# One weight load for high and low dt weights, and squares added on GpSimd ahead of one product of ones

## The chip, the cores and the metric

The kernel runs on one core of a Trainium2 chip. The metric is the device time of one execution in microseconds. Its matrix engine is called TensorE (PE in the profile), its other engines VectorE (DVE), ScalarE (ACT), GpSimd (POOL) and SyncE (SP), which issues most of the DMAs.

## The reference

Two transformer-like blocks run one after the other on 256 tokens of width 1024, in fp32. The first has sliding-window attention, a gated recurrent branch and a gated feed-forward. The second is where the change lies:

```python
h = rmsnorm_2(x, norm_mix_w) * (1 + sc_m) + sh_m
z, xbc, dt_raw, q, k, v = jnp.split(h @ w_in, IN_SPLITS_2, axis=-1)   # 512, 1024, 8, 512, 512, 512 columns
xbc = silu(causal_dwconv(xbc, conv_w) + conv_b)
dt = softplus(dt_raw + dt_bias)                                       # 8 heads
y = ssd_scan(xs * dt[..., None], dt * A, bm, cm) + d_skip[:, None] * xs
y = y.reshape(b, s, 512) * silu(z)
y_ssd = rmsnorm_2(y, norm_w)        # y * rsqrt(mean(y * y over 512) + eps) * norm_w
y_att = chunk_attention(q, k, v, rel_bias)
x = x + g_m * (concatenate([y_ssd, y_att]) @ w_out)
h = rmsnorm_2(x, norm_ffn_w) * (1 + sc_f) + sh_f
x = x + g_f * conv_ffn(h, w_up, ffn_conv_w, w_down)
```

## The kernel before

Activations stand with their channels on the partitions ("cm" tiles) and 256 tokens along the free dimension. Every large product is split into high and low parts: a weight block `w` is held as `wH`, its value rounded to the fp32r type by ScalarE, and `wL = w - wH`, made by VectorE (`L1073`, the helper `tt`). Activations are held alike, `p1H` and `p1L`. TensorE then adds three products, `wH*p1H + wH*p1L + wL*p1H` (`L1672`, `L1675`), in one bank of its accumulator memory `ps`.

Weights come in panels of four blocks of 128 rows and 512 columns. SyncE loads them into four `raw` slots, ScalarE writes `wH` (`L695`), VectorE `wL`, TensorE multiplies. A panel is split two panels ahead of its use. One list written out by hand, `timeline()`, sets the order of the work; each engine walks through it and emits its own share of each entry, with semaphores between the engines. Within an engine the order is that of its queue.

The stretch that matters runs `xs`, `bc`, `q2`, `z`, `k2`, `v2`, `oo` for the second block. Between the panels of the groups stand the smaller steps:

```python
before_evac = {"oo1": [("squares", 3)], "xs": [("dt",)], "bc": [("xdt",)]}
gemm("xs", [("h_final",)])
gemm("bc", [("dt_turn",)])
gemm("q2", [("sA", 0)], [("sC", 0), ("sA", 1)])
gemm("z", [("sY", 0), ("sC", 1)], [("sY", 1), ("yz",)])
gemm("k2", [("ysum",), ("bias",), ("snorm",)], X(6, "k2", 1))
```

*dt.* `dtw` holds the 8 dt columns of `w_in_2` for the eight 128-row blocks. In `setup` ScalarE makes `dtH` and VectorE `dtL`. In `dt`, behind the second panel of `xs`, TensorE adds 8 x 3 products into 8 partitions of bank 7 (`L1893`). VectorE copies them to `dtrow` (`L1523`). In `dt_turn`, behind the first panel of `bc`, TensorE transposes `dtrow` into two 128x8 tiles (`L1899`). VectorE and ScalarE compute softplus and `ADT = dt * A` (semaphore `adt`; `L1033`, `L1035` on ScalarE). In `xdt`, behind the second panel of `bc`, TensorE waits for the convolved `xs` (`xc_done`, ScalarE `L901`) and `adt` and then transposes `xs` (`L1601`). The next group, `q2`, writes to the banks that ScalarE empties in its evacuation of `bc` (`L820`). The convolution of `xs` is twelve VectorE instructions (`L1076`) behind `L1523` in VectorE's queue.

*The SSD norm.* In `yz` VectorE multiplies the four 128x256 tiles of `y` by `silu(z)`, and ScalarE squares each into `sT[:, t]` (`L1043`, semaphore `ysq`). In `ysum`, behind the first panel of `k2`, TensorE adds the squares over partitions and tiles by four products with a matrix of ones (`L1951`, plain fp32, so that each product appears as two passes). ScalarE takes logarithm and exponential (`L1047`, `L1049`). In `snorm` VectorE multiplies, ScalarE and VectorE make the high and low parts for `oo`. The attention scores of unit 6 (`L1800`) stand behind the second panel of `k2`; they wait for the evacuation of `k2` on ScalarE.

GpSimd makes masks and constants at the start (`step` is its helper: the instruction raises `pool_step` and the next waits for it) and later does one product and one memset for each half of the recurrent branch (`L658`, `L666`).

Of the kernel before, what the change touches and what calls it, by code (L numbers as in the profile page):

```python
# [6 lines left out]
F32 = mybir.dt.float32  # L7
F32R = mybir.dt.float32r
BF16 = mybir.dt.bfloat16
U32 = mybir.dt.uint32  # L10
ACT = mybir.ActivationFunctionType
ALU = mybir.AluOpType
AX_X = mybir.AxisListType.X

P = 128
D = 1024
KD = D // P
T = 256
# [74 lines left out]
SUM_AT = {"f3": (2, 1), "f5": (3, 1), "f7": (4, 1), "f9": (5, 1), "norm": (6, 2), "post": (8, 2)}  # L93
SUMS = list(SUM_AT)
NSUM = 32
GATE_OF = {1: 0, 3: 1}

LATER = {("down1", 5): 2, ("oo1", 1): 3}
# [99 lines left out]
def build(nc, IN, out):  # L198
# [17 lines left out]
    with ExitStack() as ctx:  # L216


        on = Signals()
# [175 lines left out]
        def sb(name, shape, dt=F32):  # L395
            return ctx.enter_context(nc.sbuf_tensor(name, shape, dt))
# [57 lines left out]
        UT = sb("UT", [P, P], BF16)  # L454
        reset = sb("reset", [P, T], BF16)
        R0, R1, Ra, Rb = (sb(n, [P, TB]) for n in ("R0", "R1", "Ra", "Rb"))
        dtrow = scr(58, T)[0:8]
        XS, YS, S2, pre = sb("XS", [P, 2, TB]), sb("YS", [P, 2, TB]), sb("S2", [P, TB]), sb("pre", [P, TB])
        XA, YA, pre2 = sb("XA", [P, 1]), sb("YA", [P, 1]), sb("pre2", [P, 1])
        fetch, fetch2 = sb("fetch", [P, 32]), sb("fetch2", [P, 1])  # L460
# [7 lines left out]
        am, af = sb("am", [P, 8]), sb("af", [P, 8])  # L468
        RM, NM, DS, ES, SU, RD = (sb(n, [P, 2, 8]) for n in ("RM", "NM", "DS", "ES", "SU", "RD"))
        E5 = sb("E5", [P, 4, 4])  # L470
        dtH, dtL = sb("dtH", [P, KD, 8], F32R), sb("dtL", [P, KD, 8], F32R)
        DT, DR, DA, DE, ADT = (sb(n, [P, TB, 8]) for n in ("DT", "DR", "DA", "DE", "ADT"))
        nega, Bs = sb("nega", [P, 8]), sb("Bs", [P, 6, 8])
        ext_dram = nc.dram_tensor("ext_dram", (8, 384), F32).ap()
# [129 lines left out]
        @block.gpsimd  # L604
        def _(pool):

            steps = [0]

            def step(ins):

                steps[0] += 1
                ins.then_inc(on.pool_step, 1)
                pool.wait_ge(on.pool_step, steps[0])

            def select(t, cond, fill, op=ALU.is_ge):

                base_, mult, stp = cond
                step(pool.affine_select(out=t, in_=t, compare_op=op, fill=fill, base=base_,
                                        pattern=[[stp, t.shape[-1]]], channel_multiplier=mult))

            step(pool.memset(eps[:], EPS))
            step(pool.memset(nega[:], 0.0))
            step(pool.memset(ident[:], 0.0))
            select(ident[:], (0, 1, -1), 1.0, ALU.not_equal)
            step(pool.memset(ones[:], 1.0))

            step(pool.memset(identb[:], 0.0))
            select(identb[:], (0, 1, -1), 1.0, ALU.not_equal)

            step(pool.memset(mask1[:], 0.0))  # L630
            select(mask1[:, 0:P], (-1, -1, 1), NEG)
            select(mask1[:, P:2 * P], (0, 1, -1), NEG)

            step(pool.memset(reset[:], 1.0))
            step(pool.memset(reset[:, 0:T:C], 0.0))

            step(pool.memset(UT[:], 1.0))
            select(UT[:], (0, -1, 1), 0.0)
            step(pool.tensor_copy(CL[:], UT[:]))
            step(pool.memset(CL[0:C, C:P], 0.0))  # L640
            step(pool.memset(SL[:], 1.0))
            select(SL[:], (-1, 1, -1), 0.0)
            step(pool.memset(OL[:], 0.0))
            step(pool.memset(OL[0:C, :], 1.0))
            step(pool.memset(M0[:], 0.0))
            step(pool.tensor_scalar(M0[:, 0:C], CL[:, 0:C], -1.0, None, ALU.mult))
            step(pool.memset(M1[:], 0.0))
            step(pool.tensor_scalar(M1[:, C:P], CL[:, C:P], -1.0, None, ALU.mult))
            step(pool.tensor_copy(M1[0:C, 0:C], SL[0:C, 0:C]))

            step(pool.tensor_copy(hmask[0:C, :], UT[0:C, 0:C]))
            step(pool.tensor_copy(hmask[C:P, :], UT[C:P, C:P]))
            pool.memset(fetch2[:], 0.0).then_inc(on.consts, 1)
            for e in TL:
                if e[0] == "hprep" and e[2] == 2:
                    pool.wait_ge(on.hE3, e[1] + 1)
                    pool.wait_ge(on.hQp, e[1] + 1)
                    pool.tensor_tensor(hQ, hQ, T2, ALU.mult).then_inc(on.hQq, 1)  # L658
                elif e[0] == "hprep" and e[2] == 3:
                    if e[1]:  # L660
                        pool.wait_ge(on.o_psum, 2 * e[1])
                    else:
                        pool.wait_ge(on.aks, 2)
                        pool.wait_ge(on.dtw_lo, 1)
                        pool.wait_ge(on.pv_psum, NU1)
                    pool.memset(hAT, 0.0).then_inc(on.hat_zero, 1)  # L666
# [3 lines left out]
        def _(act):  # L670
# [241 lines left out]
            for e in TL:  # L912
# [26 lines left out]
                    tail(e[1])  # L939
                elif k == "setup":  # L940
                    act.wait_ge(on.in_dtw, 16)
                    nc.scalar.activation(dtH[:], dtw, ACT.Copy).then_inc(on.dtw_hi, 1)
                elif k == "scores":
                    table(ACT.Exp)
                elif k == "scale":
# [115 lines left out]
        def _(dve):  # L1061
# [10 lines left out]
            def tt(o, a, b, op):  # L1072
                return v.tensor_tensor(o, a, b, op)  # L1073
# [272 lines left out]
            for e in TL:  # L1346
# [21 lines left out]
                elif k == "setup":  # L1368
# [4 lines left out]
                    step(v.memset(ext[:, 0:P - 1], 0.0))  # L1373
                    v.tensor_scalar(ext[:, 0:P - 1], ext[:, 0:P - 1], ext[:, P - 1:P], None, ALU.add).then_inc(on.ext_done, 1)
                    dve.wait_ge(on.dtw_hi, 1)
                    tt(dtL[:], dtw, dtH[:].bitcast(F32), ALU.subtract).then_inc(on.dtw_lo, 1)
                elif k == "ada":
                    q = e[1]
                    i = SIDX["ada", q]
# [140 lines left out]
                elif k == "dt":  # L1520
                    dve.wait_ge(on.h_final, TB)
                    dve.wait_ge(on.dt_raw, 1)
                    v.tensor_copy(dtrow, ps[0:8, 7, 0:T]).then_inc(on.dt_row, 1)  # L1523
                elif k == "dt_turn":
                    dve.wait_ge(on.dt_psum, 1)
                    f = lambda n: pc(n, 0, 8).unsqueeze(1).broadcast_to([P, TB, 8])
# [70 lines left out]
        def _(pe):  # L1597
# [137 lines left out]
            for e in TL:  # L1735
# [152 lines left out]
                elif k == "dt":  # L1888
                    pe.wait_ge(on.dtw_lo, 1)
                    pe.wait_ge(on.u_ready, 24)  # L1890
                    for kk in range(KD):
                        for x, (wt, at_) in enumerate(((dtH, p1H), (dtH, p1L), (dtL, p1H))):
                            last = mm(ps[0:8, 7, 0:T], wt[:, kk, :], at_[:, kk, :], start=kk == 0 and x == 0,  # L1893
                                      stop=kk == KD - 1 and x == 2)
                    last.then_inc(on.dt_raw, 1)
                elif k == "dt_turn":
                    pe.wait_ge(on.dt_row, 1)
                    for j in range(TB):
                        last = nc.tensor.transpose(ps[:, 7, 8 * j:8 * j + 8], dtrow[:, j * P:(j + 1) * P], ident[0:8, 0:8])  # L1899
                    last.then_inc(on.dt_psum, 1)  # L1900
                elif k == "xdt":
                    pe.wait_ge(on.xc_done, 1)
# [5 lines left out]
                elif k == "sA":  # L1908
                    g = e[1]
                    pe.wait_ge(on.adt, 1)  # L1910
                    if g:
                        pe.wait_ge(on.seg, g)
                    a = sc45.rearrange("p (h n) -> p h n", h=4)
                    for h in range(4):
                        for j in range(TB):
                            last = mm(a[:, h, j * P:(j + 1) * P], ADT[:, j, 4 * g + h:4 * g + h + 1].broadcast_to([P, P]),
                                      CL[:], start=True, stop=True)
                    last.then_inc(on.abc_psum, 1)
                    pe.wait_ge(on.xd, 2)
                    if g == 0:  # L1920

                        for x, terms in enumerate((((M0, 0),), ((M1, 0),), ((SL, 0),), ((SL, 0), (OL, 1)),
                                                   ((M0, 1),), ((M1, 1),))):
                            for y, (mat, j) in enumerate(terms):
                                last = mm(ps[:, 7, 64 + 8 * x:72 + 8 * x], mat[:], ADT[:, j, :], start=y == 0,
                                          stop=y == len(terms) - 1)
                        last.then_inc(on.bm_psum, 1)
                elif k == "sC":
                    g = e[1]
                    if g:  # L1930
                        pe.wait_ge(on.cb, g)
                    pe.wait_ge(on.xc_done, 2)
                    mm(ps[:, 6, 0:T], XC[:, 4 + g, 0:P], XC[:, 6 + g, :], start=True, stop=True)
                    last = mm(ps[:, 6, T:T + P], XC[:, 4 + g, P:T], XC[:, 6 + g, P:T], start=True, stop=True)
                    last.then_inc(on.cb_psum, 1)
                elif k == "sY":
                    g = e[1]
                    pe.wait_ge(on.g_done, g + 1)
                    if g:
                        pe.wait_ge(on.sy, 2 * g)  # L1940
                    for hh in range(4):
                        h = 4 * g + hh
                        o = ps[C * (hh % 2):C * (hh % 2) + C, 7, (hh // 2) * T:(hh // 2 + 1) * T]
                        mm(o, XD[:, 0, h * DH:(h + 1) * DH], SG[g][:, hh, 0:T], start=True, stop=False)
                        last = mm(o[:, P:T], XD[:, 1, h * DH:(h + 1) * DH], SG[g][:, hh, T:T + P], start=False, stop=True)
                    last.then_inc(on.sy_psum, 1)
                elif k == "ysum":
                    pe.wait_ge(on.sy, 4)
                    for t in range(4):
                        pe.wait_ge(on.ysq, t + 1)  # L1950
                        last = mm(ysum, ones[:], sT[:, t], start=t == 0, stop=t == 3)  # L1951
                    last.then_inc(on.yss, 1)


INPUTS = ["x", "w_in", "b_in", "w_branch_attn", "w_branch_hgrn", "w_out", "w_ffn_gate", "w_ffn_up", "w_ffn_down",
# [40 lines left out]
```

## Time and profile before

| | |
|---|---|
| median of three runs | 815.47 us (815.34 to 817.68) |
| profiled execution | 815.34 us, its span 813.6 us |
| TensorE busy | 796.6 us, 98% |
| VectorE busy | 592.4 us, 73% |
| ScalarE busy | 498.6 us, 61% |
| GpSimd busy | 15.8 us, 2% |
| DMA moved | 161.15 MB |

The span runs from the first to the last instruction of the profiled execution. Times of rows are microseconds from its start. An instruction's row gives start, length, engine, source line, operation, output and inputs, shape and count; in brackets stands how long the engine was idle before it, and who ended that.

### The profile page before, as it was taken

How to read it: one execution, taken by the hardware profiler on the slowest of the kernel's cores; microseconds unless marked ns; L12 is line 12 of the kernel's file. 1: busy time of each engine (PE TensorE's matmuls, PEld its weight loads, DVE VectorE, ACT ScalarE, POOL GpSimd, SP SyncE). 2: the span in 40 equal slices, each digit the busy share in tenths (PEclk: the TensorE clock that was granted, in tenths of full speed). 3: DMA queues.
4: the chain of work that ended last, by engine and by line, in shares of the span. 5: the costliest groups of instructions: out<-in, count | busy, mean ns of one | idle time of the engine just before them, and what ended most of it. 6: DMA issues, size and time to landing. Idle time of an engine off the chain costs nothing. (4 is left out here: it accounts for less than half of the span.)

```text
span 813.6 us, 14276 instructions
## 1 busy us (share of the span) xinstructions
PE 796.6 (98%) x5952; PEld 744.8 (92%) x5952; DVE 592.4 (73%) x772; ACT 498.6 (61%) x752; POOL 15.8 (2%) x36
## 2 busy tenths in 40 slices
PE   8999999999999999999999999999999999999996
PEld 8988879999999889999998889999788999999885
DVE  5575686648766877887878897897768877787463
ACT  6777788568837475344344266856657776666452
POOL 3000000000200000000000000000000000000000
PEclk9999999999999999999999999999999999999999
DMA  8873634446453577889798993635352865646611
GB/s 301 285 252 111 207 104 156 155 155 226 162 183 105 160 254 232 264 292 298 253 300 279 354 358 110 234 133 155 104 173 68 256 205 168 197 137 200 233 52 52
DMA packets 105680, 161.15 MB, mean 198 GB/s; under 512 B 4480, under 2 KB 51856, under 8 KB 105616
## 3 DMA queue, kind: packets, MB, share of 16 engines
q1 hardware_dynamic: 105472, 159.97, 59.8%
q8 instruction: 47, 0.77, 0.4%
q10 hardware_dynamic: 144, 0.26, 0.1%
q14 instruction: 17, 0.14, 0.0%
HBM read 159.16 MB, written 1.06 MB: 197 GB/s over the span
## 5 line engine op out<-in xcount | busy, mean ns | idle before, releaser
L1073 DVE TENSOR_TENSOR wL<-raw,wH 128x2048 fp32r<-128x2048 f32 (+2 forms) x134 | 283.0, 2118 | 122.7 <-ACT wH L695 119.2
L1672 PE MATMUL ps<-p1H,wH 128*128 128x256 f32 x1256 | 359.2, 286 | 1.7 <-DVE p1L L1073 0.8
L1672 PE MATMUL ps<-p1L,wH 128*128 128x256 f32 x1256 | 355.3, 283 | 0.0
L1672 PE MATMUL ps<-p1H,wL 128*128 128x256 f32 x1256 | 355.3, 283 | 0.0
L695 ACT ACTIVATE wH<-raw 128x2048 fp32r<-128x2048 f32 (+1 forms) x120 | 223.1, 1866 | 122.1 <-PE ps L1672 65.9
L1672 PEld LDWEIGHTS ps<-p1H,wH 128*128 128x128 f32 x1256 | 240.8, 192 | 4.8 <-issue 3.5
L1672 PEld LDWEIGHTS ps<-p1L,wH 128*128 128x128 f32 x1256 | 240.9, 192 | 0.3 <-issue 0.2
L1672 PEld LDWEIGHTS ps<-p1H,wL 128*128 128x128 f32 x1256 | 240.8, 192 | 0.0
L1675 PE MATMUL ps<-wH,zH 128*128 128x512 f32 x168 | 65.4, 389 | 0.0
L1675 PE MATMUL ps<-wH,zL 128*128 128x512 f32 x168 | 65.4, 389 | 0.0
L1675 PE MATMUL ps<-wL,zH 128*128 128x512 f32 x168 | 65.4, 389 | 0.0
L1076 DVE SCALAR_TENSOR_TENSOR arena<-arena,par 128x256 f32<-128x256 f32 x124 | 50.7, 480 | 9.9 <-ACT arena L886 7.6
L820 ACT ACTIVATE arena<-ps 128x256 f32<-128x256 f32 x86 | 30.5, 378 | 28.2 <-PE ps L1672 27.8
L1076 DVE SCALAR_TENSOR_TENSOR arena<-raw,cact,arena 128x512 f32<-128x512 f32 x56 | 42.1, 751 | 1.7
L1073 DVE TENSOR_TENSOR arena<-arena 128x512 f32<-128x512 f32 (+3 forms) x41 | 35.2, 872 | 6.6 <-ACT arena L841 2.6
L1675 PEld LDWEIGHTS ps<-wL,zH 128*128 128x128 f32 x168 | 31.5, 188 | 6.6
L1675 PEld LDWEIGHTS ps<-wH,zH 128*128 128x128 f32 x168 | 31.5, 188 | 6.6
L1675 PEld LDWEIGHTS ps<-wH,zL 128*128 128x128 f32 x168 | 31.5, 188 | 6.4
L1672 PE MATMUL ps<-pyH,wH 128*128 128x256 f32 x128 | 36.6, 286 | 0.0
L1672 PE MATMUL ps<-pyL,wH 128*128 128x256 f32 x128 | 36.2, 283 | 0.0
L1672 PE MATMUL ps<-pyH,wL 128*128 128x256 f32 x128 | 36.2, 283 | 0.0
L1675 PE MATMUL ps<-wH,p1H 128*128 128x512 f32 (+1 forms) x92 | 34.4, 374 | 0.0
(284 smaller groups left out, 974.5 us busy)
## 6 DMA issues: line engine op xcount, KB each, us to landing
raw<-in_w_in SPq DMA_DIRECT2D x37, 1024.0 KB, 5.1
raw<-in_w_ada SPq DMA_DIRECT2D x24, 1024.0 KB, 5.2
raw<-in_w_up SPq DMA_DIRECT2D x44, 512.0 KB, 4.8
raw<-in_w_ffn_gate SPq DMA_DIRECT2D x22, 512.0 KB, 4.5
raw<-in_w_ffn_up SPq DMA_DIRECT2D x22, 512.0 KB, 5.6
raw<-in_w_ffn_down SPq DMA_DIRECT2D x10, 1024.0 KB, 5.3
raw<-in_w_down SPq DMA_DIRECT2D x10, 1024.0 KB, 5.0
raw<-in_w_out SPq DMA_DIRECT2D x8, 1024.0 KB, 5.1
```

Of the source, the lines that this page charges most:

```text
L695: nc.scalar.activation(wH[:, q % NHL, 0:nk, 0:wd], raw[:, i % NRAW, 0:nk, 0:wd], ACT.Copy).then_inc(on.w_hi, 1)
L820: nc.scalar.activation(dst(m), ps[:, t[1], 0:T], f, **bias).then_inc(on.evac_act, 1)
L1073: return v.tensor_tensor(o, a, b, op)
L1076: return v.scalar_tensor_tensor(out=o, in0=a, scalar=s, in1=b, op0=op0, op1=op1)
L1672: last = mm(ps[:, t[1], 0:T], wt[:, slot, k, t[2]:t[2] + P], at_[:, k0 + k, :], start=st, stop=en)
L1675: last = mm(ps[:, t[1], 0:t[3]], at_[:, k0 + k, t[4] * P:(t[4] + 1) * P], wt[:, slot, k, t[2]:t[2] + t[3]], start=st, stop=en)
```

## The change

The high and the low dt weights become the two halves of one tile `dtHL` with 16 columns. TensorE loads the 16 columns at once and multiplies them with `p1H` and with `p1L`: 16 products in place of 24, whose output has 16 partitions, eight with the high and eight with the low weights. (The product low by low, which was left out before, is now in the sum.) `dtrow` has 16 partitions. In `dt_turn` the transposes become products with `pairs`, a 16x8 matrix with two ones in each column, made in `setup` on VectorE from two blocks of the identity; they turn the rows and add the two halves.

In `ysum` GpSimd waits for all four squares and adds them in two instructions, 128x512 and 128x256, and TensorE, which waits for the second, does one product of ones in place of four.

```diff
@@ -93,6 +93,7 @@
+POOL_SETUP = 27
@@ -454,7 +455,7 @@
-        dtrow = scr(58, T)[0:8]
+        dtrow = scr(58, T)[0:16]
@@ -468,7 +469,8 @@
-        dtH, dtL = sb("dtH", [P, KD, 8], F32R), sb("dtL", [P, KD, 8], F32R)
+        dtHL, pairs = sb("dtHL", [P, KD, 16], F32R), sb("pairs", [P, 8])
+        dtH, dtL = dtHL[:, :, 0:8], dtHL[:, :, 8:16]
@@ -651,8 +653,13 @@
+            assert steps[0] == POOL_SETUP, steps
             for e in TL:
-                if e[0] == "hprep" and e[2] == 2:
+                if e[0] == "ysum":
+                    pool.wait_ge(on.ysq, 4)
+                    step(pool.tensor_tensor(sT[:, 0:2], sT[:, 0:2], sT[:, 2:4], ALU.add))
+                    step(pool.tensor_tensor(sT[:, 0], sT[:, 0], sT[:, 1], ALU.add))
+                elif e[0] == "hprep" and e[2] == 2:
@@ -939,7 +946,7 @@
-                    nc.scalar.activation(dtH[:], dtw, ACT.Copy).then_inc(on.dtw_hi, 1)
+                    nc.scalar.activation(dtH, dtw, ACT.Copy).then_inc(on.dtw_hi, 1)
@@ -1373,7 +1380,8 @@
-                    tt(dtL[:], dtw, dtH[:].bitcast(F32), ALU.subtract).then_inc(on.dtw_lo, 1)
+                    tt(pairs[0:16], ident[0:16, 0:8], ident[0:16, 8:16], ALU.add)
+                    tt(dtL, dtw, dtH.bitcast(F32), ALU.subtract).then_inc(on.dtw_lo, 1)
@@ -1520,7 +1528,7 @@
-                    v.tensor_copy(dtrow, ps[0:8, 7, 0:T]).then_inc(on.dt_row, 1)
+                    v.tensor_copy(dtrow, ps[0:16, 7, 0:T]).then_inc(on.dt_row, 1)
@@ -1889,14 +1897,14 @@
                     for kk in range(KD):
-                        for x, (wt, at_) in enumerate(((dtH, p1H), (dtH, p1L), (dtL, p1H))):
-                            last = mm(ps[0:8, 7, 0:T], wt[:, kk, :], at_[:, kk, :], start=kk == 0 and x == 0,
-                                      stop=kk == KD - 1 and x == 2)
+                        for x, at_ in enumerate((p1H, p1L)):
+                            last = mm(ps[0:16, 7, 0:T], dtHL[:, kk, :], at_[:, kk, :], start=kk == 0 and x == 0,
+                                      stop=kk == KD - 1 and x == 1)
                     last.then_inc(on.dt_raw, 1)
                 elif k == "dt_turn":
                     pe.wait_ge(on.dt_row, 1)
                     for j in range(TB):
-                        last = nc.tensor.transpose(ps[:, 7, 8 * j:8 * j + 8], dtrow[:, j * P:(j + 1) * P], ident[0:8, 0:8])
+                        last = mm(ps[:, 7, 8 * j:8 * j + 8], dtrow[:, j * P:(j + 1) * P], pairs[0:16], start=True, stop=True)
                     last.then_inc(on.dt_psum, 1)
@@ -1946,10 +1954,8 @@
                 elif k == "ysum":
                     pe.wait_ge(on.sy, 4)
-                    for t in range(4):
-                        pe.wait_ge(on.ysq, t + 1)
-                        last = mm(ysum, ones[:], sT[:, t], start=t == 0, stop=t == 3)
-                    last.then_inc(on.yss, 1)
+                    pe.wait_ge(on.pool_step, POOL_SETUP + 2)
+                    mm(ysum, ones[:], sT[:, 0], start=True, stop=True).then_inc(on.yss, 1)
```

## Rows read from the trace of the kernel before

**Rows 1.** The page: busy time of engines (part 1) and TensorE's clock by slice (part 2).
```profile
PE 796.6 (98%) x5952; PEld 744.8 (92%) x5952; DVE 592.4 (73%) x772; ACT 498.6 (61%) x752; POOL 15.8 (2%) x36
...
PEclk9999999999999999999999999999999999999999
```

**Rows 2.** Waits of TensorE over the span: us in total, times, longest; eight rows.
```profile
PE ps L1601 <- DVE arena L1073: 4.4, 7, 1.1
...
PE ps L1672 <- ACT arena L820: 0.2, 1, 0.2
```

**Rows 3.** Timeline of TensorE, 507 to 524 us: start, length, line, operation.
```profile
507.93 0.28 PE L1893 MATMUL ps<-p1H,dtH 128*8 128x256 f32 x1
...
510.66 0.28 PE L1672 MATMUL ps<-p1H,wH 128*128 128x256 f32 x1
...
516.51 0.29 PE L1899 MATMUL ps<-ident,arena 8*128 8x8 f32 x2
516.73 0.39 PE L1672 MATMUL ps<-p1H,wH 128*128 128x256 f32 x1
...
522.59 1.04 PE L1601 MATMUL ps<-ident,arena 128*128 128x128 f32 x8
523.86 0.36 PE L1672 MATMUL ps<-p1H,wH 128*128 128x256 f32 x1 [0.23 <-ACT arena L820]
```

**Rows 4.** Timeline of VectorE, 506 to 522 us.
```profile
506.07 2.29 DVE L1073 TENSOR_TENSOR wL<-raw,wH 128x2048 fp32r<-128x2048 f32 x1 [2.15 <-ACT wH L695]
...
512.34 4.82 DVE L1076 SCALAR_TENSOR_TENSOR arena<-arena,par 128x256 f32<-128x256 f32 x12
517.08 2.27 DVE L1073 TENSOR_TENSOR wL<-raw,wH 128x2048 fp32r<-128x2048 f32 x1
...
521.96 0.18 DVE L1073 TENSOR_TENSOR ADT<-DT,nega 128x16 f32<-128x16 f32 x1
```

**Rows 5.** Line `L1925` on TensorE: ns min/median/max, first and last start.
```profile
L1925 PE MATMUL ps<-ADT,M x8: 175/256/256, 531.5 to 532.8; 128*128 128x8 f32 x8
```

**Rows 6.** Timeline of ScalarE, 517 to 525 us.
```profile
517.19 1.06 ACT L901 ACTIVATE arena<-arena 128x1024 f32<-128x1024 f32 x1 [3.04 <-DVE arena L1076]
...
521.55 1.90 ACT L695 ACTIVATE wH<-raw 128x2048 fp32r<-128x2048 f32 x1
523.35 1.18 ACT L820 ACTIVATE arena<-ps 128x256 f32<-128x256 f32 x4
```

**Rows 7.** Timeline of TensorE, 562 to 571 us.
```profile
562.52 1.89 PE L1951 MATMUL ps<-arena,ones 128*128 128x256 f32 x8
...
564.37 0.28 PE L1672 MATMUL ps<-p1L,wH 128*128 128x256 f32 x1
...
570.84 1.16 PE L1800 MATMUL ps<-arena 64*128 64x128 f32 x16 [0.68 <-ACT arena L820]
```

**Rows 8.** Timeline of ScalarE, 558 to 565 us.
```profile
558.27 1.42 ACT L1043 ACTIVATE arena<-arena 128x256 f32<-128x256 f32 x4 [2.61 <-DVE arena L1073]
...
562.80 0.20 ACT L677 ACTIVATE fetch<-eps 128x1 f32<-128x1 f32 x1
564.45 0.47 ACT L1047 ACTIVATE arena<-ps,eps 128x256 f32<-128x256 f32 x1 [1.45 <-PE ps L1951]
```

**Rows 9.** Timeline of GpSimd over the span.
```profile
7.28 0.37 POOL L646 TENSOR_SCALAR M<-CL 128x64 f32<-128x64 f32 x1
...
140.78 2.41 POOL L658 TENSOR_TENSOR arena<-arena 128x1024 f32<-128x1024 f32 x1 [130.89 <-ACT arena L987]
...
212.92 4.42 POOL L658 TENSOR_TENSOR arena<-arena 128x1024 f32<-128x1024 f32 x1 [68.84 <-ACT arena L987]
```

**Rows 10.** Timeline of VectorE, around 213 us and 562 us.
```profile
212.80 2.29 DVE L1073 TENSOR_TENSOR wL<-raw,wH 128x2048 fp32r<-128x2048 f32 x1
...
215.00 3.43 DVE L1073 TENSOR_TENSOR arena<-arena 128x1024 f32<-128x1024 f32 x1
...
561.53 2.29 DVE L1073 TENSOR_TENSOR wL<-raw,wH 128x2048 fp32r<-128x2048 f32 x1 [2.29 <-ACT wH L695]
```

## The prediction

> **What bounds the kernel now.** The first part of the profile page comes first: TensorE is busy for nearly the whole span, at a granted clock near its 2.4 GHz level in every slice, and VectorE, the next engine, for under three quarters [rows 1]. The waits of TensorE over the whole span make eight groups that add up to about 10 us [rows 2]. So time saved on TensorE is time saved, except where TensorE then arrives earlier at something that another engine delivers at a time of its own. The change touches two places, around 508 to 524 us (dt) and 558 to 571 us (the SSD norm). I read TensorE's timeline there, then those of VectorE and ScalarE, and asked at each wait behind the edit whether its deliverer moves too.
>
> **Setup.** One more VectorE instruction (`pairs`, 16x8) stands in front of `dtL`, early in the kernel. The work that hides it is TensorE's whole stream up to 507.93, where `dtL` is first used [rows 3]; without that cover it would cost its own length, about 0.2 us, like the 128x16 product at 521.96 [rows 4]. The 16-column store of `dtH` is the same work in another layout. GpSimd's `POOL_SETUP` is only a count.
>
> **dt products.** The 24 products start at 507.93, and the panel `bc` behind them at 510.66 [rows 3]: 2.73 us, 0.114 us each. The change issues 16, with 16 weight columns for 8. I take the same 0.114 us: the moving side, 256 columns, is the same, and even with 128 weight columns the 48 products of a panel go at 0.12 us (516.73 to 522.59 is 5.86 us [rows 3]). 0.12 is the upper bound. TensorE saves 8 x 0.114 = 0.91 us (at the bound, 2.73 - 1.92 = 0.81).
>
> **Turning dt.** Two transposes become two plain fp32 products of 8 columns. Before: 516.51 to 516.73, 0.22 us [rows 3]. Small fp32 products with 128-wide weights are at `L1925`: 14 passes start from 531.5 to 532.8, 0.1 us a pass, two passes a product [rows 5]. So 2 x 0.2 = 0.4 us, that is +0.2 us; bounds 0 (if they go like the transposes) and +0.3. Up to here TensorE is 0.7 us ahead.
>
> **Where those 0.7 us go.** The VectorE queue does not follow TensorE here. It starts the low split of `bc` at 506.07, behind a ScalarE instruction, before the dt products begin, and from there runs without idle time: two splits, the dt row copy, twelve convolution steps from 512.34 and the next split from 517.08 [rows 4]. The dt row is wanted at 512, and TensorE was done at 510.7; arriving 0.9 us sooner changes nothing. ScalarE waits 3.04 us for the convolution, then does its silu, two table loads and the dt exponential and logarithm; the product `ADT` ends at 521.96 + 0.18 = 522.14 in either kernel [rows 4, 6]. TensorE reached the `xdt` transposes at 522.59, 0.45 us later than that. With 0.7 us less to do it would be there at 521.9 and has to wait for `ADT` until about 522.2: 0.3 to 0.4 us is left. Behind the transposes `q2` needs the bank that ScalarE's evacuation of `bc` frees. That evacuation stands in ScalarE's queue behind a weight split (521.55) and begins at 523.35; TensorE already waited 0.23 us for it, until 523.86 [rows 3, 6]. Nothing in that queue waits for what the dt edit makes earlier. So `q2` starts at 523.86 still, the wait grows from 0.23 to about 0.6 us, and **the dt edit is worth 0**. Its bounds: 0, and 0.7 us if the evacuation does move.
>
> **ysum.** Four fp32 products of ones, recorded as eight passes. They start at 562.52, and the second product of `k2`'s second part stands at 564.37; at the pace of 0.12 us the first effectively stood at 564.25 [rows 7]. That is 1.73 us for eight passes, 0.216 us a pass, in which the change from one kind of product to the other and back is held too, and that stays. One product has two passes, so six go: 1.30 us at most, and with 0.02 us of it for the change of kind I take **1.28 us**.
>
> **The two additions on GpSimd.** They wait for the fourth square, which ends at 558.27 + 1.42 = 559.69 [rows 8]. They are the last entries of GpSimd's queue; nothing is queued behind them. Its only such operation before is the 128x1024 product of `L658`: 2.41 us once, 4.42 us the other time [rows 9]. The slow one (212.92) started while a split of 2.29 us ran on VectorE, and the VectorE instruction behind that took 3.43 us [rows 10]. In my window VectorE is idle for 2.29 us, until the split that ScalarE frees at 561.53 [rows 10], so the fast row counts. Without a fixed part it gives 2.35 ns an element: 1.20 us for 512 and 0.60 for 256. The fixed part is at most the 0.37 us that a 64-element operation takes [rows 9], which gives 1.39 and 0.88. By the slow row it would be 2.21 and 1.10. I take 1.3 and 0.75. ScalarE's logarithm follows the end of ysum by 0.04 us (562.52 + 1.89 to 564.45 [rows 7, 8]); I allow 0.08 us for each such step: first 559.77 to 561.07, second 561.15 to 561.90, TensorE free to go at 561.98. It arrives at 562.52 in either kernel. The cover is 0.5 us; by the high bounds (562.20) 0.3 us. If it were gone, each 0.1 us of lateness would cost 0.1 us. The second addition may still hold VectorE's split (561.53) for 0.4 us; that split is used by `v2`, behind the scores at 570.84 [rows 7], and what VectorE does next in the norm needs ScalarE's exponential, after 563.17 (below), so this is free.
>
> The Trainium skill says (SBUF — State Buffer, Who interferes with whom) that a VectorE instruction with two SBUF inputs and a GpSimd instruction that reads SBUF exclude each other for a whole instruction, whichever starts first. The trace agrees: from 212.92 GpSimd is held until the split ends at 215.09, and the 2.25 us that remain of its 4.42 are near the 2.41 us of the other row. It is the rule that speaks against this change; by it the sum stays at 1.28 us as long as the second addition starts before 561.53, as I have it.
>
> **Does the 1.28 us last?** The table for the logarithm is in place at 562.80 + 0.20 = 563.0; the sum would come at 564.45 - 1.28 = 563.17 [rows 8], still behind the table. Logarithm, exponential, VectorE's four products and ScalarE's four copies hang in one chain on that sum, and the evacuation of `k2`, on which the scores wait 0.68 us at 570.84 [rows 7], stands behind them and behind TensorE's own `k2`; both sides move by 1.28 us. I saw no wait for a DMA behind 560 us. SP's loads wait for splits and move with them. So the whole rest moves.
>
> **Sum.** Span 813.6 - 1.28 - 0 = 812.3 us. The profiled execution took 815.34 us beside its span of 813.6, so 815.34 - 1.28 = 814.06. The median of the runs shown is 815.47, 0.13 above it. I say **814.1 us**, 0.17% faster than the median, which lies inside the 0.3% (2.4 us) that a measurement of this kernel can tell from no change.
>
> **Rivals.**
> *Both edits pay* (0.10). The 0.7 us at dt survives, because the evacuation at 523.35 follows something I don't see. For it: TensorE is at 98%. Against: the 0.23 us wait and a VectorE queue without a gap [rows 3, 4]. Time 815.34 - 1.98 = 813.4.
> *GpSimd misses its slot; slower* (0.10). Place: the second addition. Price: the addition waits as `L658` did at 212.92, here from 561.53 to the split's end at 563.82, and ends at 564.6 and TensorE starts at 564.7 [rows 7, 10], 2.2 us later than now; 2.2 - 1.28 = +0.9, so 816.3. It decides from the point at which the first addition ends after 561.45, that is takes over 1.68 us, against my 1.3 and high bound 1.39. For it: the 4.42 us row [rows 9]. Against: an empty VectorE at its start. The Trainium skill (GPSIMD Engine Reference, Elementwise — side-by-side cycle accounting) has 4497 ns for 2048 elements; with the row here that is a fixed part near 0.3 us, an estimate from that page, inside my bounds.
> *Nothing arrives* (0.08). Half-hidden additions, or a later wait that does not move (the table at 563.0 is only 0.17 us away), eat the 1.28 us: 815.3.
> The forecast has 0.72.
>
> **Numbers.** The forecast's own range is 813.7 to 814.6, from the bounds of the passes and of the additions and some 0.3 us that the runs shown differ by (the two lower ones by 0.13). The range for 8 in 10 takes in the first rival (813.4) and the third (815.3), each with as much again for the runs, and leaves out the second: 813.2 to 815.9. Faster by over 0.3% (below 813.0) needs more than both edits together give: 0.06. Slower by over 0.3% (above 817.9) needs more than the second rival's price, such as a still longer GpSimd stall: 0.04. Within: 0.90.
>
> **What would show it.** dt: 16 products, `bc` 0.9 us earlier, the wait in front of `xdt` or of `q2` larger by as much in total, `q2` and everything up to 562 us at the same time of the span. ysum: two GpSimd records, about 1.3 and 0.75 us, both done before 562.4, no wait of TensorE at ysum, two passes there, and the scores' products 1.28 us sooner. I am wrong if `q2`'s first product moves (the dt edit then pays), if the second addition shows over 2 us, or if the wait before the scores grows.

## The result and the profile after

The changed kernel took 814.36 us (median of 22 executions, 813.64 to 818.68), the kernel before, in the same sessions, 815.89 us (22 executions, 815.05 to 818.60). The ratio is 0.998, with a 95% interval of 0.9971 to 0.999. Forecast were 814.1 us and 0.17% less than before; by the medians it is 0.19% less. The profiled execution took 814.24 us with a span of 812.5, against 815.34 and 813.6.

The page of the changed kernel, parts 1 and 2, beside [rows 1]: TensorE does 1.6 us less, GpSimd 2.1 us more.

```profile
PE 795.0 (98%) x5940; PEld 743.6 (92%) x5940; DVE 592.6 (73%) x773; ACT 498.7 (61%) x752; POOL 17.9 (2%) x38
...
PEclk9999999999999999999999999999999999999999
```

TensorE's timeline of the changed kernel through the dt stretch, beside [rows 3]:

```profile
508.13 0.28 PE L1901 MATMUL ps<-p1H,dtHL 128*16 128x256 f32 x1
...
509.95 0.28 PE L1680 MATMUL ps<-p1H,wH 128*128 128x256 f32 x1
...
515.80 0.61 PE L1907 MATMUL ps<-pairs,arena 16*128 16x8 f32 x4
516.33 0.38 PE L1680 MATMUL ps<-p1H,wH 128*128 128x256 f32 x1
...
522.06 0.28 PE L1680 MATMUL ps<-p1H,wL 128*128 128x256 f32 x1
522.48 1.06 PE L1609 MATMUL ps<-ident,arena 128*128 128x128 f32 x8
524.06 0.36 PE L1680 MATMUL ps<-p1H,wH 128*128 128x256 f32 x1 [0.52 <-ACT arena L827]
524.25 0.28 PE L1680 MATMUL ps<-p1L,wH 128*128 128x256 f32 x1
```

Follow the lead of the changed kernel over the one before, start by start. The dt products begin 0.20 us later (508.13 for 507.93), because TensorE waited 0.19 us longer for VectorE in the norm in front of `xs`, here first before, then after:

```profile
493.50 0.49 PE L1605 MATMUL ps<-ident,R 128*128 128x128 f32 x2 [0.17 <-DVE R L1127]
```

```profile
493.70 0.49 PE L1613 MATMUL ps<-ident,R 128*128 128x128 f32 x2 [0.36 <-DVE R L1134]
```

At the first product of `bc` the changed kernel is 0.71 us ahead, so the dt products saved 0.91. Behind the turning it is 0.40 ahead: the turning costs 0.31 more. At the `xdt` transposes 0.11 is left, and at `q2` it is 0.20 us behind, exactly where it stood in front of dt. Counted from there, the lead was 0.91, 0.60, 0.31 and 0.00. The loss at `xdt` stands in no bracket, only in the starts: 0.42 us from 522.06 to 522.48, where the kernel before takes 0.12. The wait before `q2` has grown from 0.23 to 0.52.

The two queues that deliver there, VectorE and then ScalarE, each from its timeline of the changed kernel, beside [rows 4] and [rows 6]. All rows lie 0.19 to 0.20 us behind those of before:

```profile
506.27 2.29 DVE L1080 TENSOR_TENSOR wL<-raw,wH 128x2048 fp32r<-128x2048 f32 x1 [2.15 <-ACT wH L702]
...
522.15 0.17 DVE L1080 TENSOR_TENSOR ADT<-DT,nega 128x16 f32<-128x16 f32 x1
```

```profile
521.75 1.90 ACT L702 ACTIVATE wH<-raw 128x2048 fp32r<-128x2048 f32 x1
523.55 1.19 ACT L827 ACTIVATE arena<-ps 128x256 f32<-128x256 f32 x4
```

GpSimd's timeline from 300 us on, TensorE's around ysum and the scores (beside [rows 7]), VectorE's at 562 us (beside [rows 10]), all of the changed kernel:

```profile
559.98 1.31 POOL L660 TENSOR_TENSOR arena<-arena 128x512 f32<-128x512 f32 x1 [341.75 <-ACT arena L1050]
561.36 0.74 POOL L661 TENSOR_TENSOR arena<-arena 128x256 f32<-128x256 f32 x1
```

```profile
562.73 0.60 PE L1958 MATMUL ps<-arena,ones 128*128 128x256 f32 x2
...
563.28 0.28 PE L1680 MATMUL ps<-p1L,wH 128*128 128x256 f32 x1
...
569.74 1.16 PE L1808 MATMUL ps<-arena 64*128 64x128 f32 x16 [0.68 <-ACT arena L827]
```

```profile
561.73 2.52 DVE L1080 TENSOR_TENSOR wL<-raw,wH 128x2048 fp32r<-128x2048 f32 x1 [2.29 <-ACT wH L702]
```

The additions end at 562.10, TensorE comes to ysum at 562.73 and waits for nothing. VectorE's split is held up by 0.23 us (2.52 for 2.29), which nobody waits for. Behind ysum `k2`'s second product is 1.09 us ahead of before, from 0.21 us behind in front of it: a gain of 1.30 us. The scores are 1.10 us ahead and their wait is the same 0.68. That is the difference of the spans, 1.1 us.

### The profile page after: what moved, and what is told of

Same layout as the page of the kernel before. It is cut to its first block and busy times, and to the rows that moved or that the text cites. A ratio compares the mean times of both kernels' runs of the same rounds, so it can differ in the third digit from the quotient of the medians.

```text
span 812.5 us, 14256 instructions
## 1 busy us (share of the span) xinstructions
PE 795.0 (98%) x5940; PEld 743.6 (92%) x5940; DVE 592.6 (73%) x773; ACT 498.7 (61%) x752; POOL 17.9 (2%) x38
## 3 DMA queue, kind: packets, MB, share of 16 engines
HBM read 159.16 MB, written 1.06 MB: 197 GB/s over the span
```

## The experiments

My theory: the ysum edit gives 1.3 us and the dt edit nothing, because TensorE's earlier arrival ends in waits on VectorE's `ADT` and ScalarE's evacuation of `bc`. Rivals: both edits pay; or GpSimd's additions are a cost in some other way. Every time is a median of 12 executions (e10: 7, e11: 10) with its range in brackets; "before" is the kernel before, executed in the same session. The sessions are e1 to e4, e5 to e8, e9 and e10, e11 and e12.

**e1, the dt edit alone.** From the changed kernel, ysum put back and the GpSimd additions taken out:

```diff
-                    pe.wait_ge(on.pool_step, POOL_SETUP + 2)
-                    mm(ysum, ones[:], sT[:, 0], start=True, stop=True).then_inc(on.yss, 1)
+                    for t in range(4):
+                        pe.wait_ge(on.ysq, t + 1)
+                        last = mm(ysum, ones[:], sT[:, t], start=t == 0, stop=t == 3)
+                    last.then_inc(on.yss, 1)
```

> The dt edit alone, ysum as before. My theory (the dt edit is absorbed by waits that others set): ratio 1.000 to before, q2's first product at the same time of the span as before, counted from the norm in front of it, and its wait on ScalarE's evacuation 0.5 us in place of 0.23. Rival (both edits pay): 0.6 us less, ratio 0.9993, with q2 earlier by 0.6 us.

Measured: 816.52 us (814.87 to 819.41) against 816.61; ratio 0.9997, interval 0.9982 to 1.0012. The fastest execution of this kernel took 814.87 us, that of before 814.77. The ratio fits my theory, but does not exclude 0.9993. The waits could not be read as expected, for another thing had happened in the profiled execution. TensorE's row per stretch (us, busy time and instructions, granted clock, DMA share, GB/s), first of e1, then of the kernel before:

```profile
493.00:496.00 3.00, 2.78 (x20) 0.83 0.00 1
496.00:499.00 3.00, 3.00 (x16) 0.50 0.00 0
499.00:502.00 3.00, 3.00 (x17) 0.53 0.03 5
```

```profile
493.00:496.00 3.00, 2.83 (x26) 1.00 0.01 2
496.00:499.00 3.00, 3.00 (x28) 1.00 0.00 0
499.00:502.00 3.00, 3.00 (x28) 1.00 0.03 5
```

In e1 the granted clock fell to 0.50, the 1.2 GHz level, in the norm in front of `xs`, during the second of two groups of 32-column products, and TensorE was 3.1 us late when it came back. VectorE's queue was less late; its convolution of `xs`, on which both deliveries hang, started 1.14 us later than in [rows 4]:

```profile
513.48 4.82 DVE L1079 SCALAR_TENSOR_TENSOR arena<-arena,par 128x256 f32<-128x256 f32 x12
```

So what the others deliver there lay ready when TensorE came, and the dt edit does show: 3.12 us behind before dt, 2.21 after the products, 2.52 after the turning, 2.05 at `q2`'s second product, with no wait at `xdt` or `q2`. Of that 1.07 us, 0.91 - 0.31 = 0.60 is the edit's and 0.47 is the wait of the kernel before, which falls away when TensorE is late (e5 below gives its size).

**e2, the ysum edit alone.** The GpSimd additions and the single product put into the kernel before.

> The ysum edit alone, dt as before. My theory: it carries all of the gain, ratio 0.998 to 0.9985 (1.3 us), and every start of a product before 562 us is as before. Rival (the dt edit carries part): the gain is under 1.0 us, and the dt edit alone has the rest.

Measured: 814.78 us (813.92 to 816.96) against 816.61; ratio 0.9983, 0.997 to 0.9995. The fastest took 813.92 against 814.77. Here too the clock fell (1.5 us were lost between 490 us and dt), so that the starts before 562 us are not those of before. From the first dt product to `q2`'s second product, with the old dt, this late TensorE made good 0.48 us, the wait of before alone, against 1.07 in e1. ysum itself brought 1.28 us.

**e3, the last addition made late.** One more GpSimd addition in between, whose result is not used:

```diff
                     step(pool.tensor_tensor(sT[:, 0:2], sT[:, 0:2], sT[:, 2:4], ALU.add))
+                    step(pool.tensor_tensor(sT[:, 2], sT[:, 2], sT[:, 3], ALU.add))
                     step(pool.tensor_tensor(sT[:, 0], sT[:, 0], sT[:, 1], ALU.add))
...
-                    pe.wait_ge(on.pool_step, POOL_SETUP + 2)
+                    pe.wait_ge(on.pool_step, POOL_SETUP + 3)
```

> The changed kernel with a third GpSimd addition (128x256, of two tiles that are no longer needed, result unused) between the two. It takes 0.74 us, so that the last addition would start at about 562.2 us, behind the start of VectorE's weight split (561.7). If VectorE and GpSimd exclude each other for whole instructions, the last addition waits for the end of that split, about 564.0, and ends at 564.8; TensorE waits at ysum for about 2.1 us and the kernel is 0.8 us slower than before (ratio 1.001). If the filler starts before the split and only it and the last addition follow each other freely, the last addition ends at 562.95 and TensorE waits 0.25 us: 1.0 us faster than before (0.9988).

Measured: 817.98 us (815.73 to 818.81) against 816.61; ratio 1.0011, 1.0001 to 1.0022. GpSimd's, VectorE's and TensorE's timelines of e3:

```profile
559.67 1.31 POOL L660 TENSOR_TENSOR arena<-arena 128x512 f32<-128x512 f32 x1 [341.54 <-ACT arena L1051]
561.06 0.74 POOL L661 TENSOR_TENSOR arena<-arena 128x256 f32<-128x256 f32 x1
561.87 2.65 POOL L662 TENSOR_TENSOR arena<-arena 128x256 f32<-128x256 f32 x1
```

```profile
561.43 2.52 DVE L1081 TENSOR_TENSOR wL<-raw,wH 128x2048 fp32r<-128x2048 f32 x1 [2.29 <-ACT wH L703]
```

```profile
564.67 0.96 PE L1959 MATMUL ps<-arena,ones 128*128 128x256 f32 x2 [2.09 <-POOL arena L662]
```

The same operation takes 0.74 us when it starts before VectorE's split and 2.65 us when it starts behind it: it ends 0.57 us after the split. So a GpSimd addition and this VectorE instruction do not share: but for some 0.15 us, one waits for the other's end. The Trainium skill says that such a pair contends (SBUF — State Buffer, Who interferes with whom), a VectorE instruction with two SBUF inputs and a GpSimd instruction that reads SBUF. The fastest execution, 815.73, is 0.96 us above the fastest of before, near the expected 0.8. The median is 1.4 us above, and the stretches of the profiled execution say why: behind the wait the clock fell, at a place where it fell in no other profile.

```profile
563.00:566.00 3.00, 1.33 (x5) 0.82 0.31 29
566.00:569.00 3.00, 3.00 (x19) 0.61 0.83 321
```

In that profile TensorE was 1.1 us later than before at the first product behind ysum and 2.5 us later from 568 us on (counted from 0.11 us ahead at 562). TensorE was free to start ysum 2.25 us later than it otherwise would have, and the edit gives 1.28 to 1.30 back, so the wait costs 0.96; the other 1.6 us of the 2.6 are the clock's.

**e4, the evacuation of `bc` first.** ScalarE evacuates `bc` before it splits `q2`'s second panel, VectorE splits it behind `xdt`. Two lines are shown; besides, `("bc", 1)` joins the list `BESIDE`, which takes the split out of its old place, and `evac` can emit its four copies alone:

```diff
-    before_evac = {"oo1": [("squares", 3)], "xs": [("dt",)], "bc": [("xdt",)]}
+    before_evac = {"oo1": [("squares", 3)], "xs": [("dt",)], "bc": [("xdt",), ("evac0",), ("split", "bc", 1)]}
+                elif k == "evac0":
+                    evac("bc", True)
```

> The changed kernel, with ScalarE's evacuation of bc in front of the weight split of q2's second panel, and on VectorE that split behind xdt. My theory: the wait of 0.5 us before q2 goes; the xdt transposes are still held by adt (about 0.3 us of the dt edit's gain stays lost), so q2 starts 0.5 us sooner and the kernel is 1.8 us faster than before (ratio 0.9978). Rival (the wait only moves, to sA or sY, which stand behind VectorE's queue): the time is that of the changed kernel, 0.998.

Measured: 814.74 us (813.04 to 817.22) against 816.61; ratio 0.9983, 0.997 to 0.9995. The ratio does not decide; the median is 1.9 us and the fastest, 813.04, 1.7 us under those of before, near the 1.8 expected. The profiled execution was again one with a fallen clock, so that it does not show which wait went.

**e5, e4's reordering, and `xdt` without its wait on `adt`.**

```diff
                     pe.wait_ge(on.xc_done, 1)
-                    pe.wait_ge(on.adt, 1)
+                    pe.wait_ge(on.dt_abs, 1)
```

> As the kernel with bc's evacuation first, and the xdt transposes wait for dt_abs (VectorE has read dt from the bank that they overwrite) in place of adt. My theory: both waits behind the dt edit are gone, and where TensorE runs at full clock the kernel is 1.28 + 0.60 + 0.23 = 2.1 us faster than before: ratio 0.9974, its fastest execution at about 812.8 against 814.8 of before. Rival (the wait moves to sA, sC or sY): the time is that of the changed kernel, 0.998, and the profile shows a new wait of TensorE between 524 and 560 us.

Measured: 814.79 us (813.08 to 816.53) against 816.89; ratio 0.9979, 0.9968 to 0.999. The median is 2.1 us under that of before, the fastest 1.6 (813.08 for 814.72), and no faster than e4's: the times do not tell what the `adt` wait alone is worth. The clock held in the norm in this profile (0.997 over the span), and it shows both waits gone:

```profile
522.33 1.03 PE L1614 MATMUL ps<-ident,arena 128*128 128x128 f32 x8
523.12 0.36 PE L1685 MATMUL ps<-p1H,wH 128*128 128x256 f32 x1
523.32 0.28 PE L1685 MATMUL ps<-p1L,wH 128*128 128x256 f32 x1
```

It comes to dt 0.35 us behind before, and is 0.73 ahead at `q2`'s second product: 1.08 us, where 0.60 and 0.23 add up to 0.83. The 0.23 was too small: from the first transpose to `q2`'s second product e5 takes 0.99 us, the kernel before 524.05 - 522.59 = 1.46. The wait that is shown as 0.23 us delayed TensorE by 0.47. No new wait stands between 524 and 560 us. At ysum it gains 1.29 more, 2.37 in all. The changed kernel's 0.52 is too small by the same amount: from 522.48 to 524.25 is 1.77 us, 0.78 more than in e5. With the 0.30 at `xdt` its waits cost 1.08 us.

**e6, the same with the old dt.** e5's reordering and the ysum edit put into the kernel before.

> The same reordered kernel with the ysum edit but with the old dt: 24 products and transposes. My theory: the wait of 0.23 us goes, TensorE has 0.60 us more to do than with the new dt, so it is 1.5 us faster than before (0.9982) and 0.6 us slower than the reordered kernel with the new dt. Rival (the dt edit is worth nothing even with its waits gone): the two are equal.

Measured: 815.14 us (813.47 to 816.63) against 816.89; ratio 0.9977, 0.9965 to 0.999. By the medians the two are 0.35 apart, by the fastest 0.39, by the ratios not at all: the spread is too wide for 0.6 us. The starts do tell: from the first dt product to `q2`'s second product e6 takes 15.65 us and e5 15.04, 0.61 less, so with its waits gone the dt edit is worth its 0.60 on that stretch.

**e7, the additions on VectorE**, in place of GpSimd, behind its products:

```diff
+                elif k == "yadd":
+                    dve.wait_ge(on.ysq, 4)
+                    step(tt(sT[:, 0:2], sT[:, 0:2], sT[:, 2:4], ALU.add))
+                    tt(sT[:, 0], sT[:, 0], sT[:, 1], ALU.add).then_inc(on.consts, 1)
...
-                    pe.wait_ge(on.pool_step, POOL_SETUP + 2)
+                    pe.wait_ge(on.consts, 2)
```

> The changed kernel with the two additions on VectorE, which is idle from 559.2 to 561.5 us, in place of GpSimd. 0.69 and 0.42 us with a wait between them: done at about 560.9, a microsecond before GpSimd's. My theory (the additions are hidden in either place): the time is that of the changed kernel, 0.998, and no wait at ysum. Rival (GpSimd's additions cost something through the shared read path, or VectorE's in its queue): they differ by over 0.3 us.

Measured: 814.85 us (813.71 to 817.97) against 816.89; ratio 0.998, 0.9967 to 0.9993, the ratio of the changed kernel; the fastest is 813.71 for 813.64. Its profile has 1.28 us gained at ysum. GpSimd is not what brings the gain; fewer passes are.

**e8, the dt products twice.**

```diff
-                        for x, at_ in enumerate((p1H, p1L)):
+                        for x, at_ in enumerate((p1H, p1L, p1H, p1L)):
```

> The changed kernel with each of the 16 dt products done twice (dt comes out doubled), 32 products: 1.82 us more work on TensorE than in the changed kernel. My theory (a slack of 0.23 us before and 0.83 in the changed kernel ahead of q2): 0.83 of it is hidden and 1.0 us shows, 0.3 us faster than before, ratio 0.9996; no wait before q2. Rival (no slack; all dt work counts): 1.8 us slower than the changed kernel, 1.0005.

Measured: 816.30 us (814.30 to 818.88) against 816.89; ratio 0.9992, 0.9977 to 1.0007. The profile settles what the ratio leaves open. `q2` follows the transposes without a wait:

```profile
523.65 1.04 PE L1609 MATMUL ps<-ident,arena 128*128 128x128 f32 x8
524.44 0.36 PE L1680 MATMUL ps<-p1H,wH 128*128 128x256 f32 x1
524.64 0.28 PE L1680 MATMUL ps<-p1L,wH 128*128 128x256 f32 x1
```

It comes to dt 0.14 us ahead of before and is 1.07 behind when the turning is done: 1.21 us more work than before, and 1.81 more than the changed kernel, which had gained 0.60 there. At `q2`'s second product it is 0.59 behind, so 0.73 shows. Of 1.21 us, 0.48 was hidden against before, and of 1.81, 1.08 against the changed kernel. That is the slack measured by adding work, and it agrees with the 0.47 and 1.08 of e5, found by taking the waits away. Expected were 0.83 of slack and 0.3 us less than before; the slack was larger.

**e9, idle products in the norm in front of `xs`.** The fallen clock had spoiled half the comparisons. This one adds eight products, whose result is not used, between the small ones:

```diff
+            def busy(count):
+                for _ in range(count):
+                    mm(ps[:, 1, 0:T], zH[:, 0, 0:P], zH[:, 0, :], start=True, stop=True)
...
                     if n == 2:
                         ada_sum("norm")
+                        busy(3)
...
+                        if n == 2 and j == 0:
+                            busy(2)
...
                         ada_sum("post")
+                        busy(3)
```

> The changed kernel with eight idle products (128x256, result unused) among the small products of the norm in front of xs, 491 to 496 us. In four of seven profiles so far TensorE's granted clock fell to half there for up to 6 us, behind a stretch of 32-column products. If it falls because TensorE does too little in that stretch, the eight products (about 0.96 us, 0.2 to 0.4 of it inside waits) keep it up: the fastest execution is 0.6 us slower than the changed kernel's, about 814.3, but the median is nearer to it, 815.0, with the ratio to before 0.998. Rival (the clock falls for another reason): the spread stays, and the kernel is 0.6 to 1.0 us slower than the changed one, ratio 0.9988.

Measured: 814.27 us (813.72 to 815.21) against 817.04 (814.95 to 818.22); ratio 0.9971, 0.9961 to 0.9982. The spread shrank from over 3 us to 1.5. The mean granted clock over the span was 0.997 or more in all 12 executions, where 9 of 18 of before lay under it. From the norm's first transposes (490 us) to the first dt product TensorE takes 18.34 us, the changed kernel 17.83: 0.51 us of the 0.96 came through. They stand in front of dt, so the slack ahead of `q2` takes in most of them: e9 is 0.42 us behind before at dt and 0.01 behind at `q2`. That is why the fastest execution is 0.1 us above that of the changed kernel, not 0.6.

**e10, e5 with the idle products.**

> The reordered kernel with dt_abs in place of adt, and the same eight idle products. If they hold the clock: ratio 0.9975, best median of all; if not, 0.9985, behind the reordered kernel without them.

Measured: 813.57 us (813.32 to 814.44) against 817.04; ratio 0.9964, 0.9951 to 0.9977, the best of all. It is 0.70 us under e9, by the profiles 0.67 (15.04 against 15.71 us from the first dt product to `q2`'s second).

**e11 and e12, the worth of each edit with the clock held.** The idle products in the kernel with the ysum edit and the old dt (e11), and in the kernel before (e12).

> The ysum edit and the eight idle products, dt as before the change. With the clock held, the worth of the dt edit is the difference to the changed kernel with idle products (median 814.27). My theory: the dt edit is worth nothing there: 814.3. Rival: it is worth its 0.6 us: 814.9.

> The kernel before with the eight idle products only. My theory: 1.3 us above the one with the ysum edit, 815.6, with a spread of about 1.5 us in place of 4; ratio to before 0.9987, so that over half of what the filled kernels gain in the median comes from the clock. Rival (the products and not the clock explain the gain over before, or the ysum edit brings more than 1.3 us): under 815.0 or over 816.2.

Measured: e11 814.24 us (813.68 to 817.07), ratio 0.9971, 0.9956 to 0.9986; e12 815.42 us (814.94 to 816.43), ratio 0.9985, 0.9975 to 0.9996; before 816.48 in that session. The three filled kernels differ in nothing else: before 815.42, with ysum 814.24, with ysum and dt 814.27. The ysum edit is worth 1.18 us, within one session. The dt edit is worth -0.03 us, but e9 ran in another session, and drawing the runs of the two again and again leaves some 0.4 us either way, an estimate. One of e11's ten executions, 817.07, had a clock of 0.995 again. The idle products alone brought 1.06 us (e12), less than half of what e11 gained in the median (2.24), where over half was expected.

The profiles tell what the medians leave open. From the first dt product to `q2`'s second product TensorE took:

| | old dt | new dt |
|---|---|---|
| order as before, clock held | 16.12 (before) | 16.12 (changed), 16.11 (e3) |
| the same with the idle products | 15.72 (e12), 15.72 (e11) | 15.71 (e9) |
| waits gone: TensorE late by a fallen clock, or reordered, or both | 15.64 (e2), 15.65 (e6) | 15.05 (e1, e4), 15.04 (e5, e7, e10) |

In the first two rows the dt edit changes nothing, in the third it gives 0.60 us.

## Why the prediction was right, step by step

- **dt products**: 0.114 us each, 0.91 us saved. Measured 0.91.
- **Turning dt**: +0.2 us, bound +0.3. Measured +0.31. The term was mis-sized by 0.1: the four passes took 0.13 us each (515.80 to 516.33, the start of the next product), not the 0.1 us of `L1925`.
- **Where the 0.7 us go**: `q2` was to start at the same time. It did, counted from the start of dt, and e8 and e5 show the slack from both sides. Behind the wait for `ADT` 0.31 us was left, where 0.3 to 0.4 was forecast. The table above puts the edit's worth at 0 while the clock holds. One size was off: the wait "shown as 0.23 us" stood for 0.47, so there was more to be had from removing it than I thought. This did not touch the forecast, in which `q2` stays where it is.
- **ysum**: 1.28 us. Measured 1.30 in the changed kernel, 1.28 to 1.29 in e2, e5 and e7, 1.18 by the medians of e12 and e11.
- **The additions**: 1.3 and 0.75 us, done at 561.98. Measured 1.31 and 0.74, done at 562.10 in a queue that stood 0.20 later.
- **Does it last**: the scores and all behind them moved by the whole amount, their wait stayed at 0.68, which e2 and e5 show too.
- **The sum**: 814.1 us forecast, 814.36 measured. The forecast had no term for the clock. It fell in the norm in front of `xs` in many executions (in five of the nine profiles of kernels without the idle products, e1 to e8 and the changed one; the text on e9 says four of seven), and executions of one kernel lie up to 5 us apart. It did not touch both kernels alike: 9 of 22 executions of before lay over 1.5 us above its own fastest, 5 of 22 of the changed one. So the medians are 1.53 us apart, 0.25 more than the forecast, while the faster halves, with medians of 815.33 and 814.08, are 1.25 apart. The mechanism was right; that the medians came so near owes something to luck, as in the four later sessions the median of before was 816.5 to 817.0.
- **Rivals**: "both edits pay" is false while the clock holds. In the profiles with a fallen clock TensorE is late, nothing waits there, and the dt edit is worth its 0.60 us (e1, e4 and e7 against e2 and e6); how much that adds to the median I could not resolve (0.9997, 0.9982 to 1.0012). "GpSimd misses its slot" was right in its mechanism and its point of decision (e3), and in its price (+0.9) only for the fastest execution (+0.96). The profiled one took 2.4 us more in the span, since the clock fell behind the wait, and 9 of 12 took over 817.7 us. "Nothing arrives" is false: the whole gain reached the scores.

## What to carry to other kernels

Work removed from the engine that bounds a kernel pays only as far as the next thing it waits for: look for the first wait behind the edit and ask whether the one who ends it would come sooner. Here two edits of the same kind, 8 products less and 3 less, were worth nothing and 1.2 us, and the trace of before said so. Before small gains are compared, find out what makes the executions differ from one another; eight idle products, at 0.5 us, took the spread from over 3 us to 1.5 and the median down by 1.1 us (e12), where the whole change brought 1.5.

## What the runs showed of the hardware

- The granted clock fell from 1.00 to 0.50, from the 2.4 to the 1.2 GHz level, in the norm in front of `xs` in some executions and not in others of the same kernel, though TensorE was busy there for 2.78 of 3 us by its records (e1). What it did there was products of 32 columns and transposes. The wait shown among them does not tell the two apart: at most 0.22 us in e1, e2, e4 and e7, which fell, 1.27 in e6, which fell, 0.43 in e5, which did not. Eight products of 256 columns among them kept it at 1.00 in all four profiles and cost 0.51 to 0.55 us (e9 against the changed kernel, e12 against before); of 41 executions with them one, in e11, was again over 1.5 us above its kernel's fastest. Why it falls in one execution and not in the next stays open.
- Behind a wait of 2.09 us (e3) the clock fell to 0.50 as well, from about 565 to 568.3 us.
- A wait of TensorE that the profile gives as 0.23 us had delayed the next products by 0.47: in the changed kernel 0.52 stood for 0.78, in e9 0.44 for 0.67. The end of a product in the profile is modelled, and the idle time is counted from it. The distance between two starts, compared with the same pair where nothing waits, gives the true size.
- A 128x256 fp32 addition on GpSimd took 0.74 us in front of a VectorE instruction with two SBUF inputs and 2.65 behind its start; the VectorE instruction took 2.52 in place of 2.29 when GpSimd was there first.
- 16 weight columns in place of 8 changed the pace of the products by nothing that shows (0.114 us).
